# Three norm sums placed inside the slab that follows, and the shared rotary key as one slab of stacked halves, copied to four heads by ScalarE

## The reference, cut to what matters

```
def rmsnorm(x, g):
    inv = lax.rsqrt(jnp.mean(xf * xf, axis=-1, keepdims=True) + RMS_EPS)
    return (xf * inv).astype(x.dtype) * g

def mla_shared_kv(h, positions, kv_norm, w_kv_a, ckv_norm, w_uk, w_uv):
    hn = rmsnorm(h, kv_norm)
    a = hn @ w_kv_a                                   # 256 latent columns + 32 rotary columns
    c_kv = rmsnorm(a[..., :KV_RANK], ckv_norm)
    k_rope = rope(a[..., KV_RANK:][:, :, None, :], positions)
    k_nope = jnp.einsum('bsr,rhd->bshd', c_kv, w_uk)
    v = jnp.einsum('bsr,rhd->bshd', c_kv, w_uv)
    k = jnp.concatenate([k_nope, jnp.broadcast_to(k_rope, (B, S, MLA_HEADS, MLA_ROPE))], axis=-1)
    return k, v
```

## Time and profile before

| | |
|---|---|
| Median of 3 runs | 1003.12 us (1002.19 to 1003.37) |
| Profiled execution, its own time | 1002.32 us |
| Its span | 1000.6 us |
| Granted TensorE clock | 0.999 of full speed |
| TensorE busy | 990.0 us, 99% of the span |
| VectorE busy | 709.7 us, 71% |
| ScalarE busy | 603.7 us, 60% |
| GpSimd busy | 58.7 us, 6% |

### The profile page before, as it was taken

How to read it: one execution, slowest core, us unless ns; L and a number is a source line. 1 busy time by engine, 2 the same in 40 slices (tenths; PEclk the granted TensorE clock), 3 DMA queues, 4 the chain that set the end, 5 groups by cost and what they waited for, 6 DMA issues and landing times.

```text
span 1000.6 us, 19705 instructions
## 1 busy us (share of the span) xinstructions
PE 990.0 (99%) x7192; PEld 920.4 (92%) x7192; DVE 709.7 (71%) x1357; ACT 603.7 (60%) x1088; POOL 58.7 (6%) x79
## 2 busy tenths in 40 slices
PE   8999999999999999999999999999999999999997
PEld 7999999999999999899999999999999999999996
DVE  4668877776666668676496666668988596666665
ACT  6677567665555556565485555557768585555553
POOL 4011110210000002000020000002100010000000
PEclk9999999999999999999999999999999999999999
DMA  7743545365555554434445555554666455555531
GB/s 294 278 146 111 163 157 177 141 212 189 189 189 185 182 185 165 152 121 142 154 164 180 184 186 189 189 189 132 200 197 210 132 173 185 185 189 189 189 126 43
DMA packets 50904, 174.05 MB, mean 174 GB/s; under 512 B 6304, under 2 KB 8864, under 8 KB 50720
## 3 DMA queue, kind: packets, MB, share of 16 engines
q1 hardware_dynamic: 49664, 172.12, 51.9%
q10 hardware_dynamic: 1184, 1.18, 0.6%
HBM read 169.86 MB, written 1.05 MB: 171 GB/s over the span
## 4 chain that ended last, share of the span: by engine, by line
PE 95%; DVE 2%; ACT 1%; DMA 1%; issue 0%; SPq 0%; DVEq 0%
PE bank L426 94%; PE bank L640 1%; DVE arena L1470 1%; DMA stage<-slab_dram 1%; DVE a_pair L1496 0%; DVE w_lo L1477 0%; DVE xT L1507 0%; ACT soft_p L1109 0%; SPq L337 0%; DVE soft_p L1596 0%; DVE arena L1860 0%; ACT L1250 0%; DVE soft_s L1568 0%; ACT w_hi L1001 0%; ACT a_pair L1052 0%
## 5 line engine op out<-in xcount | busy, mean ns | idle before, releaser
L426 PE MATMUL bank<-a_pair,w_hi 128*128 128x256 f32 (+1 forms) x1992 | 536.8, 341 | 2.4 <-DVE w_lo L1477 1.9
L426 PE MATMUL bank<-a_pair,w_lo 128*128 128x256 f32 x1488 | 417.1, 281 | 0.0
L1477 DVE TENSOR_TENSOR w_lo<-stage,w_hi 128x1024 fp32r<-128x1024 f32 (+2 forms) x322 | 387.4, 1210 | 10.1 <-ACT w_hi L1001 5.1
L426 PEld LDWEIGHTS bank<-a_pair,w_hi 128*128 128x128 f32 x1992 | 342.3, 190 | 48.6 <-DVE w_lo L1477 4.0
L426 PE MATMUL bank<-arena_r,w_hi 128*128 128x256 f32 x1792 | 328.4, 284 | 0.0
L426 PEld LDWEIGHTS bank<-a_pair,w_lo 128*128 128x128 f32 x1488 | 282.6, 190 | 0.0
L426 PEld LDWEIGHTS bank<-arena_r,w_hi 128*128 128x128 f32 x1792 | 278.4, 191 | 4.4 <-issue 1.4
L426 PE MATMUL bank<-arena_r,w_lo 128*128 128x256 f32 x896 | 252.7, 283 | 0.0
L1001 ACT ACTIVATE w_hi<-stage 128x1024 fp32r<-128x1024 f32 x192 | 202.1, 1055 | 32.3 <-PE bank L426 32.3
L1017 ACT ACTIVATE w_hi<-stage 128x1024 fp32r<-128x1024 f32 (+2 forms) x126 | 128.3, 1027 | 81.2 <-PE bank L426 70.5
L426 PEld LDWEIGHTS bank<-arena_r,w_lo 128*128 128x128 f32 x896 | 171.0, 191 | 0.0
(11 more groups left out here) (181 smaller groups left out, 662.4 us busy)
## 6 DMA issues: line engine op xcount, KB each, us to landing
stage<-slab_dram SPq DMA_DIRECT2D x319, 512.0 KB, 4.0
con<-con_dram SPq DMA_DIRECT2D x1, 1153.5 KB, 10.5
xT<-xT_dram SPq DMA_DIRECT2D x4, 256.0 KB, 5.0
arena<-arena ACTq DMA_DIRECT2D x1, 1024.0 KB, 8.7
arena<-tmp SPq DMA_DIRECT2D x32, 32.0 KB, 3.0
out_dram<-arena SPq DMA_DIRECT2D x3, 256.0 KB, 2.5
tmp<-arena SPq DMA_DIRECT2D x16, 16.0 KB
vec<-vec_dram SPq DMA_DIRECT2D x1, 213.5 KB, 11.4
```

Of the source, the lines that this page charges most:

```text
L426: return nc.tensor.matmul(out, lhsT, rhs, start=start, stop=True, skip_group_check=True)
L1477: return nc.vector.tensor_tensor(out, a, hi.bitcast(f32), ALU.subtract)
```

## The change

Four things are edited.

1. `norm_sum` of m = 3, 4 and 5 is issued inside the slab after it, ahead of that slab's block k = 2 (`SUM_AT`). For m = 1 it stays ahead of the slab.
2. For m = 5 GpSimd adds all 7 squares, and TensorE issues one matmul of ones and not two.
3. Slab DQ+8 (`KROPE`) is packed: of each block of 128 columns only the 64 used ones are split, `w_hi` in columns 0 to 64 and `w_lo` in columns 64 to 128 of the same block. TensorE issues two matmuls a block (by hi, by lo of the activations); the result's rows 0 to 64 are the hi part and rows 64 to 128 the lo part. ScalarE copies rows 0 to 64 to partitions 64 to 128 of `tmp`, DVE adds the two, and the 8 small operations read that sum from SBUF.
4. `rope_keys`: ScalarE copies `k_rope` to heads 0 to 3 of `mla_k`, then issues the transfer for the other 12 heads, in pieces of 4 KB that it reads from those four. `mla_scores(0)` waits for the copy, `mla_scores(2)` for the transfer.

```diff
 WARM = 6
+SUM_AT = 2
 EPS = 1e-6
...
 GAP = UV + 2
+KROPE = KVA + 2
 UQ = GAP + 1
...
                              "krope_ready"))
+        krope_near = sem("krope_near")
         uq_rope = [sem(f"uq_rope{i}") for i in range(8)]
+        rope_moved, rope_summed = sem("rope_moved"), sem("rope_summed")
         fin_made, pool_added = sem("fin_made"), sem("pool_added")
...
             return t[:, uq_slab(step) % SLOTS, 0:6 * P].rearrange("p (b h c) -> p h b c", b=6, h=heads)
+
+        def rope_parts(n):
+
+            w = w_hi[:, n % SLOTS, :].rearrange("p (k c) -> p k c", c=P)
+            raw = stage[:, n % SLOTS, :].rearrange("p (k c) -> p k c", c=P)[:, :, 64:128]
+            return w[:, :, 0:64], w[:, :, 64:128], raw
...
-            def column_slab(n, slot, out, hi=a_hi, lo=a_lo, kv=False):
+            def column_slab(n, slot, out, hi=a_hi, lo=a_lo, kv=False, sums=None):
...
                 for k in range(NC):
+                    if sums and k == SUM_AT:
+                        norm_sum(sums)
                     if kv:
...
                     last = by_weights(slot, k * P, out, hi[:, k, :], lo[:, k, :], k == 0)
+                last.then_inc(slab_done, 1)
+
+            def stacked_slab(n, out, hi, lo):
+
+                pe.wait_ge(lo_made, n + 1)
+                for k in range(NC):
+                    w = w_hi[:, n % SLOTS, k * P:k * P + P]
+                    mm(out, w, hi[:, k, :], k == 0)
+                    last = mm(out, w, lo[:, k, :], False)
                 last.then_inc(slab_done, 1)
...
                 pe.wait_ge(in_con, 16)
-                if m == 5:
-
-                    last = add_index(m) + 6
-                    pe.wait_ge(sq_added, last)
-                    mm(half(7, 0), ones, sumsq[:, :], True)
-                    pe.wait_ge(sq_made, last + 1)
-                    mm(half(7, 0), ones, span(sq, last % 2 * TOK, TOK), False).then_inc(sum_done, 1)
-                    return
                 pe.wait_ge(sq_added, add_index(m) + 7)
...
                     pe.wait_ge(uk_taken, 1)
-                    pe.wait_ge(krope_ready, 16)
+                    pe.wait_ge(krope_near, 1)
                     pe.wait_ge(latcol_ready, 1)
                     pe.wait_ge(uq_nope, 4)
+                if k == 2:
+                    pe.wait_ge(krope_ready, 16)
                 if k == 4:
...
-            def wide_slab(n, slot, out):
+            def wide_slab(n, slot, out, sums=None):
...
                 for k in range(NC):
+                    if sums and k == SUM_AT:
+                        norm_sum(sums)
                     w = slice(k * P, k * P + P)
...
                 first_column_slabs(base, [half(4, 0), half(5, 0)], 2 * f + 1)
-                norm_sum(2 * f + 1)
-                wide_slab(base + 2, (base + 2) % SLOTS, bank[6])
+                if f == 0:
+                    norm_sum(1)
+                wide_slab(base + 2, (base + 2) % SLOTS, bank[6], 2 * f + 1 if f else None)
                 pe.wait_ge(r_ready, 2 * f + 2)
...
                 elif 2 <= i < 6:
-                    column_slab(n, n % SLOTS, lat_bank(i))
+                    column_slab(n, n % SLOTS, lat_bank(i), sums=4 if i == 2 else None)
+                elif i == 8:
+                    stacked_slab(n, lat_bank(i), b_hi, b_lo)
                 elif i >= 6:
                     column_slab(n, n % SLOTS, lat_bank(i), b_hi, b_lo, kv=i == 6)
-                if i == 1:
-                    norm_sum(4)
                 if i == 6:
...
                         hi, raw = uq_packed(w_hi, step), uq_raw(step)
+                    elif m == KROPE:
+                        hi, _, raw = rope_parts(m)
                     else:
...
                     latent_split(i)
+                if i == 8:
+                    act.wait_ge(slab_done, n + 1)
+                    nc.scalar.activation(tmp[64:128, 1, :], lat_bank(i)[0:64, :], ACT.Copy).then_inc(rope_moved, 1)
                 next_hi(n)
...
                 act.wait_ge(rope_ready, 2)
-                nc.scalar.dma_start(mla_k[64:128, :, :],
-                                    k_rope[64:128, :].unsqueeze(1).to_broadcast([64, HEADS, TOK])
+                near = mla_k[64:128, 0:4, :]
+                nc.scalar.activation(near, k_rope[64:128, :].unsqueeze(1).to_broadcast([64, 4, TOK]), ACT.Copy
+                                     ).then_inc(krope_near, 1)
+                act.wait_ge(krope_near, 1)
+                nc.scalar.dma_start(mla_k[64:128, 4:HEADS, :].rearrange("p (r h) t -> p r (h t)", h=4),
+                                    near.rearrange("p h t -> p (h t)").unsqueeze(1).to_broadcast([64, 3, 4 * TOK])
                                     ).then_inc(krope_ready, 16)
...
                         parts = uq_packed(w_lo, step), uq_raw(step), uq_packed(w_hi, step)
+                    elif m == KROPE:
+                        hi, low_part, raw = rope_parts(m)
+                        parts = low_part, raw, hi
                     else:
...
                 if i == 8:
-                    b = lat_bank(8)
-                    dve.wait_ge(slab_done, n + 1)
+                    both = tmp[64:128, 1, :]
+                    dve.wait_ge(rope_moved, 1)
+                    nc.vector.tensor_tensor(both, lat_bank(8)[64:128, :], both, ALU.add).then_inc(rope_summed, 1)
+                    dve.wait_ge(rope_summed, 1)
                     dve.wait_ge(r_ready, 5)
-                    own, other, sign = b[64:96, :], b[96:128, :], con[96:128, C_COLS + 2:C_COLS + 3]
+                    own, other, sign = tmp[64:96, 1, :], tmp[96:128, 1, :], con[96:128, C_COLS + 2:C_COLS + 3]
                     for r, of, at, op in ((slice(64, 96), q_cos, q_sin, ALU.add), (slice(96, 128), q_sin, q_cos, ALU.subtract)):
...
             add_squares(add_index(5) - 1, 1, 7)
-            add_squares(add_index(5), 6, 8)
+            add_squares(add_index(5), 7, 8)
             pool.wait_ge(fin_squared, 6)
```

## The result

The changed kernel takes 1004.87 us (median of 20 runs, 1004.22 to 1006.93), the kernel before in the same comparison 1003.13 us (20 runs, 1002.19 to 1004.64): a ratio of 1.0020, 95% interval 1.0014 to 1.0026, so 1.74 us slower. The forecast was 1004.5, range 1002.7 to 1005.6. The profiled execution has a span of 1002.8 us against 1000.6, at a granted clock of 0.999 in both.

A forecast was written before the change was run, and what follows sets the result against it. TensorE was taken to bound the kernel for 95% of the span. The terms 0.43 + 0.43 + 0.40 + 0.13 summed to +1.39 us, giving a median of 1004.5 us (+0.14%), range 1002.7 to 1005.6.

The forecast's parts named there:

- Sums m = 3 and m = 4: Slabs FFN2+2 and DQ+2: the wait for `w_lo` stays and the sum is added inside the slab, +0.43 us each.
- Sum m = 5: Slab FFN3+2: TensorE waits for `w_lo`, -0.03 us, then one sum inside the slab, +0.43; together +0.40 us.
- the wait ended, as in the other places 0.06 later, at 809.36: FFN3+2: TensorE's wait ends 0.06 us after `w_lo` is done at 809.30, in the changed kernel too.
- it waits for nothing there: FFN3+2, block k = 2: GpSimd's 0.74 us seventh addition is done at 808.77, TensorE arrives at 810.18; no stall.
- `w_lo` moves with the sum: Sign that the prediction is wrong; it expected slabs FFN2+2, DQ+2 and FFN3+2 to start 0.06 us after `w_lo` as before.
- The second matmul of ones: m = 5, before FFN3+2: the matmul removed was covered by the wait for all but 0.03 us.
- After the sums: Behind m = 5: second pass and `rB` 1.1 us later, at most 0.2 us of stall at FFN3+4, taken as 0.
- Rotary key: DQ+8: -0.96 us on TensorE becomes a wait before `values_slab(2)`; `keys_out(0)` comes 0.08 to 0.18 later, taken as +0.13 us.
- The first rival: The rotary key's slab keeps its gain: up to 1.26 - 0.96 = +0.3 us, 1003.4 us; chance 0.14.
- Keys of the heads: Copy and 12-head transfer before `mla_scores(0)`: TensorE did not wait for the transfer, so 0 us.
- The rival of the late transfer: Rotary query rows land 1.5 us later, TensorE stands 1.1 us at `mla_scores(0)`: +2.5 us, 1005.6 us; chance 0.14.

The follow-up runs named there:

- e9: The kernel before, unchanged, measured against itself: 1002.75 us against 1003.67, ratio 0.9993.
- e1: Kernel before with only the sums of m = 3 and m = 4 moved inside the following slab: 1003.62 us against 1003.52, ratio 1.0000.
- e2: Kernel before with seven GpSimd additions and one matmul of ones for m = 5, sum at its old place: 1003.53 us against 1003.52, ratio 1.0002.
- e5: Kernel before with the rotary key's part, plus two `w_lo` subtractions moved behind `keys_out(0)`: 1002.51 us against 1003.81, ratio 0.9988.
- e11: Kernel before with ScalarE's copy to four heads, then the 12-head transfer in 768 pieces of 1 KB: 1002.61 us against 1003.67, ratio 0.9992.
- e6: Kernel before with only ScalarE's copy to four heads and the 12-head transfer in 192 pieces of 4 KB: 1002.33 us against 1003.81, ratio 0.9988.
- e10: Repeat of e6 (copy to four heads, 192 pieces of 4 KB) against the kernel before: 1002.86 us against 1003.67, ratio 0.9995.
- e3: Kernel before with the sum of m = 5 inside the following slab, still six additions and two matmuls: 1003.58 us against 1003.52, ratio 1.0006.
- e7: Kernel before with m = 3 and 4 sums inside the slab at block 5, seventh addition held until `w_lo` is made: 1003.51 us against 1003.81, ratio 0.9999.
- e4: Kernel before with the rotary key's part alone (packed slab, copy, 12-head transfer), sums as before: 1002.86 us against 1003.52, ratio 0.9994.
- e12: Kernel before with the 12-head transfer in 768 pieces of 1 KB, issued ahead of ScalarE's copy: 1002.58 us against 1003.67, ratio 0.9991.

## Why the prediction came out as it did

The total was right, and in part by luck. Against the trace it is off by +0.54 us: +0.46 for m = 5 and +0.20 for a step at the end, less 0.11 at m = 3, with 0.02 or less elsewhere. That stays inside the 0.6 us allowed for the forecast, and the median (1004.87, forecast 1004.5) cannot tell it from a hit, since two medians of one kernel lay 0.92 apart (e9).

**Sums m = 3 and m = 4.** Right in mechanism: the sums had stood in a wait that is there anyway, `w_lo` did not move, and the sum was added to the slab. m = 4 cost +0.44 (e1 +0.46), forecast +0.43. m = 3 cost +0.32, in e1 too. The missing 0.11 is not shown to belong to the edit: e2, e5 and e11, which leave m = 3 alone, regain 0.11 to 0.13 over the same slabs.

**Sum m = 5.** This is the term that was mis-sized: +0.86, not +0.40. The step that failed reads "the wait ended, as in the other places 0.06 later, at 809.36": I kept that release point for the changed kernel, because I costed GpSimd's seventh addition by its own 0.74 us and by when TensorE needs its result ("it waits for nothing there"). I did not ask what the addition does to the instruction beside it. It makes `w_lo` 0.55 us longer, and `w_lo` is what TensorE waits for (e2: +0.52 by that alone; 0.03 less, because the second sum had held TensorE that long). With the sum's 0.43 that would be +0.95; the trace has +0.86, and 0.10 is what e6, e10 and e11 regain here without an edit. The prediction named as a sign of being wrong that `w_lo` moves with the sum. Its end did move, but e3 shows that it goes with the addition. The rows to see it in were on the table: `w_lo` takes 1.77 and 1.70 (1.76 counted from its own start; the chain of rows 6 counts from the end of the instruction before) with seven additions and 1.21 with six, for the same 128 x 1024 subtraction. I read the three as given durations and not as two cases.

The Trainium skill, "SBUF — State Buffer", section "Who interferes with whom", says that a VectorE instruction with two SBUF inputs contends with a GpSimd instruction that reads SBUF, that whichever issues first holds the shared ports for its whole instruction, and that the other blocks. `w_lo` reads `stage` and `w_hi`, the addition reads `sumsq` and `sq`. The traces agree in both directions: where GpSimd was first by 0.06 us it took 0.74 and VectorE 1.76 (changed kernel, e2), where VectorE was first GpSimd took 1.56 and VectorE 1.21 (e7). A `w_lo` that had to do all of its 1.21 us behind the addition would end 1.21 behind it; it ends 1.08 behind, so some 0.13 of it overlaps.

**The second matmul of ones.** Right: it was covered. e3, which keeps it and pays both inside the slab, costs +0.83 against +0.86. Taking it away saved 0.43 us of TensorE inside the slab and needed one more GpSimd addition, which cost 0.52.

**After the sums.** Taken as 0, right. `rB` of m = 5 came at 812.46 instead of 809.70, 1.66 later against the drift of 1.10, where 1.1 was forecast, and FFN3+4 did not wait. e7 shows where that ends: between 1.4 and 2.0 us for m = 3.

**Rotary key.** Right in mechanism: +0.11 against +0.13. Two small misreadings cancel in it. The first of the eight operations starts 0.51 us later (719.61 against 718.11, less the drift of 0.99), not 0.39 to 0.49. And VectorE's list had 0.41 us to give, not 0.31: the small operations ahead of `keys_out(0)` start 0.07 us apart, so it could have started at 727.48 + 0.07 = 727.55 and not only when the last of them had ended. The two rows of the kernel before:

```profile
727.41 0.17 DVE L2047 TENSOR_SCALAR small<-small 128x2 f32<-128x2 f32 x1
727.48 0.16 DVE L2048 TENSOR_SCALAR small<-small 128x2 f32<-128x2 f32 x1
```

Reading the sum from `tmp` where the bank was read shortened nothing, as taken: 0.42 us before and after. e4 shows the same by itself (+0.11), and e5 that the gain comes back up to `values_slab(2)` if VectorE's list is shortened. The first rival, that the slab keeps its gain, is out for this kernel.

**Keys of the heads.** Right at 0 against the profile that it was read from (e6, e10 in their traces). The rival of the late transfer is out: less the drift of 0.99, the fourth rows land 0.8 us earlier than before, not later, and TensorE starts `mla_scores(0)` 1.2 us behind them in the changed kernel.

**What no term held.** From the last slab to the end the changed kernel loses 0.20 us. VectorE's scaling of the output starts later behind ScalarE's `rB`, 1.59 us of idle where the kernel before has 1.22:

```profile
995.81 2.56 DVE L1506 TENSOR_TENSOR arena<-arena,rB 128x256 f32<-128x256 f32 x5 [1.59 <-ACT rB L1051]
```

(e4; the kernel before has this row:)

```profile
994.97 2.64 DVE L1470 TENSOR_TENSOR arena<-arena,rB 128x256 f32<-128x256 f32 x5 [1.22 <-ACT rB L1022]
```

It is in the three kernels with the rotary slab's edit (changed, e4, e5) and in none of the other eleven profiles. No wait in the trace explains it, and no experiment was made on it: its cause is open. So is that of the scatter of the start (TensorE's first slab ends 0.03 to 1.12 us later than in the kernel before, over thirteen profiles), which can be more than half of the change.

No kernel here is shown to be faster than the kernel before. The intervals of e5 (0.9980 to 0.9997) and e6 (0.9979 to 0.9996) lie below 1. But in e5's trace the change itself comes to nothing (0.94 ahead of DQ+8, 0.93 at the end), e6 has the span of before, and e9 shows 0.9 us for nothing.

## What to carry to other kernels

When an edit adds an instruction on GpSimd, look up what VectorE runs at that moment, and whether TensorE waits for it: the price is not on GpSimd's line. When the same operation on the same shape has two durations in a profile (1.21 and 1.76 here), find what separates them before using either as a constant. A gain on the bounding engine lasts only to the next event that another engine's list sets, so measure that list's slack first (0.4 us here, for a gain of 0.96); and for effects of 0.1% compare matching events in two traces, and run the old kernel against itself before reading a median.

## What the runs showed of the hardware

- A VectorE subtraction of 128 x 1024 (two inputs in SBUF, 1.21 us alone) takes 1.76 us when GpSimd's 128 x 256 addition starts 0.06 us ahead of it; it then ends 1.08 us behind the addition, in thirteen profiles, and in e7 too, where the addition had started 0.89 us ahead. In the other order the addition takes 1.56 us instead of 0.74, and that `w_lo` keeps its 1.21.
- SBUF to SBUF, 768 KB in pieces of 1 KB took 8.6 us to landing (e11), in pieces of 4 KB 7.9 and 8.7 (e6, e10). Issued 1.2 us ahead of the slab load in the other queue the transfer took 7.0 and that load 7.7 (e12); issued 0.2 ahead, 7.9 to 8.7 and 4.0 to 4.9 (six profiles).
- The same kernel, measured twice in one session with 11 and 33 runs, had medians 0.92 us apart.
